# First products of the local attention in the linear attention's tail, and GpSimd's query low parts two heads ahead

## The reference, cut to what matters

```python
h = rmsnorm(x, norm_mix_g)
proj = h @ w_in            # linear attention q, k, v, r; local attention sq, sk, sv; two gates
o_a = rmsnorm(gla_chunked(gq, gk, gv, log_a)) * silu(gr)          # 4 heads of 128/256
q = partial_rope(rmsnorm(sq), cos, sin)                            # 16 heads of 64
k = partial_rope(rmsnorm(sk), cos, sin)                            # 4 key/value heads of 64
o_b = swa_sink_attention(q, k, sv, sinks)                          # window of 128
x = x + (sigmoid(gate_a) * (o_a @ w_a) + sigmoid(gate_b) * (o_b @ w_b)) @ w_out
# expert layer, 8 heads: the 16 best of 128 + 128 keys, then the 16 best of their 256 sums
qp = rmsnorm(x) @ w_pq
s_top, i_top = top_k(qp . sub_keys, 16)
best, pos = top_k(s_top[0][:, None] + s_top[1][None, :], 16)
x = x + sum_over_chosen(softmax(best) * gelu(x . u[idx]) * v[idx])
```

## Time and profile before

| | |
|---|---|
| median of three runs | 3020.08 us (3020.02 to 3022.21) |
| the profiled execution | 3024.87 us, its span 3023.1 us |
| mean granted clock of TensorE | 0.974 |
| TensorE busy | 2831.7 us (94%) |
| VectorE busy | 1832.2 us (61%) |
| ScalarE busy | 1207.7 us (40%) |
| GpSimd busy | 664.7 us (22%) |

### The profile page before, as it was taken

One profiled execution on the slowest core, in us unless ns is written; L12 is line 12 of the kernel. 1 busy time (PEld: TensorE's weight loads), 2 busy tenths in 40 slices (PEclk: granted clock), 3 DMA queues, 4 the chain that ended last, 5 costly groups with the idle time before them and its releaser, 6 DMA issues. The chain is left out here.

```text
span 3023.1 us, 39247 instructions
## 1 busy us (share of the span) xinstructions
PE 2831.7 (94%) x14634; PEld 2440.4 (81%) x14634; DVE 1832.2 (61%) x3340; ACT 1207.7 (40%) x2121; POOL 664.7 (22%) x400
## 2 busy tenths in 40 slices
PE   7989989989989999898999999899969988999998
PEld 6889558788989989897888888788757767888877
DVE  4434643369988888676788887644924554344432
ACT  3433642333337767332333333467424442222221
POOL 0013210023332333364232332043022310000000
PEclk9999999999999999999999999999979999999999
DMA  3202112344347988899999999467365531322232
GB/s 126 84 21 80 51 58 88 139 137 141 127 129 258 314 303 311 322 400 367 353 360 354 362 359 353 177 200 217 125 192 157 142 138 48 114 96 96 97 105 70
DMA packets 251468, 572.34 MB, mean 189 GB/s; under 512 B 43616, under 2 KB 152032, under 8 KB 222272
## 3 DMA queue, kind: packets, MB, share of 16 engines
q1 hardware_dynamic: 212160, 426.56, 42.1%
q0 software_dynamic: 36864, 134.23, 11.4%
q10 hardware_dynamic: 2304, 9.70, 0.9%
HBM read 486.38 MB, written 84.02 MB: 189 GB/s over the span
## 5 line engine op out<-in xcount | busy, mean ns | idle before, releaser
L44 PE MATMUL pe_ps<-hh,pe_uh 128*128 128x384 f32 x1024 | 349.8, 342 | 16.1 <-issue 13.6
L46 PE MATMUL pe_ps<-hh,pe_ul 128*128 128x384 f32 x1024 | 344.1, 336 | 0.0
L45 PE MATMUL pe_ps<-hl,pe_uh 128*128 128x384 f32 x1024 | 344.0, 336 | 0.0
L44 PE MATMUL pe_ps<-pe_vh,pe_whi 128*128 128x512 f32 x768 | 300.1, 391 | 6.5 <-DVE pe_vl L1721 6.5
L45 PE MATMUL pe_ps<-pe_vl,pe_whi 128*128 128x512 f32 x768 | 299.8, 390 | 0.0
L46 PE MATMUL pe_ps<-pe_vh,pe_wlo 128*128 128x512 f32 x768 | 299.7, 390 | 0.0
L1546 POOL DMA_INDIRECT pe_gu<-in_u_rows,pe_urow x128 | 198.8, 1553 | 304.6 <-DVE pe_gu L1682 287.5
L1554 POOL DMA_INDIRECT pe_gv<-in_v_w,pe_vrow x128 | 158.6, 1239 | 332.7 <-DVE pe_acc L1691 320.8
L44 PEld LDWEIGHTS pe_ps<-hh,pe_uh 128*128 128x128 f32 x1024 | 193.8, 189 | 18.2 <-issue 17.8
L1682 DVE SCALAR_TENSOR_TENSOR pe_gu<-pe_gu,pe_xs 128x1024 f32<-128x1024 f32 x128 | 155.0, 1218 | 86.1 <-DMA pe_gu<-in_u_rows,pe_urow 85.7
L45 PEld LDWEIGHTS pe_ps<-hl,pe_uh 128*128 128x128 f32 x1024 | 193.9, 189 | 0.3
(11 more groups left out here) (595 smaller groups left out, 6986.5 us busy)
## 6 DMA issues: line engine op xcount, KB each, us to landing
xu<-in_u_w SPq DMA_DIRECT2D x64, 1024.0 KB, 6.3
pe_v_raw<-in_v_w SPq DMA_DIRECT2D x64, 1024.0 KB, 8.5
hidden_scratch<-pe_hs SPq DMA_DIRECT2D x64, 384.0 KB, 8.5
gate_scratch<-pe_stage SPq DMA_DIRECT2D x24, 1024.0 KB, 11.2
pe_hw<-hidden_scratch SPq DMA_DIRECT2D x64, 384.0 KB, 4.6
pe_gate<-gate_scratch SPq DMA_DIRECT2D x64, 384.0 KB, 5.3
gf_raw<-in_gdn_w SPq DMA_DIRECT2D x16, 1024.0 KB, 6.8
gb_pk<-pk_scratch SPq DMA_DIRECT2D x64, 256.0 KB, 2.8
```

The source lines that it names most:

```text
L44: pe.matmul(out, lh, rh, start=start, stop=False)
L45: pe.matmul(out, lh, rl, start=False, stop=False)
L46: return pe.matmul(out, ll, rh, start=False, stop=stop)
```

## The change

- `gla`: it gets the banks (`ps`) of the local attention instead of its own. Behind the last head's products TensorE waits for the next phase's high weights (`nxt.w_hi`) and makes the products with them (`swa_high`: 16 a token tile) of three tiles, then the transposes, then the fourth tile's. SyncE also loads the raw weights of the local attention's head 1 into the one raw buffer, when head 0's are split on both engines.
- `swa_heads`: project(0) makes only the products with the low weights; project(1) makes its 64 products with the high weights before it waits for the low ones, then 32 with these. Head 2's raw weights have a buffer of their own (`sh_raw2`, in memory that the attention's output takes later) and a semaphore of their own, and are issued first in the phase, ahead of the small tables. Head 3's are loaded when head 1's are split.
- `peer`, GpSimd: the low part of head 1 first; then for head h the candidate sums, the low part of head h+2, the one-hot product.
- `peer`, VectorE: the low part of expert block 2h+3 goes behind the pick and ahead of the candidates' search (before, it stood behind the search in heads 0 to 6, and ahead of the pick in head 7). In head 7 block 19's, which stood behind the pick of head 7, goes ahead of the comparison.

```diff
@@ gla
             @block.sync
                 sp.wait_ge(w_lo, 2 * GLA_H)
                 sp.dma_start(nxt.raw[:], nxt.src).then_inc(nxt.raw_in, 16)
+                sp.wait_ge(nxt.w_hi, 1)
+                sp.wait_ge(nxt.w_lo, 1)
+                sp.dma_start(nxt.raw[:], nxt_src).then_inc(nxt.raw_in, 16)
...
                 steps(pe, GLA_H, step)
-                turn(GLA_H * NT)
+                pe.wait_ge(nxt.w_hi, 1)
+                for n in range(NT):
+                    swa_high(pe, ps, hh, hl, nxt.wh, n)
+                    if n == 2:
+                        turn(GLA_H * NT)
+def swa_high(pe, ps, hh, hl, wh, n):
+    rows = slice(n * P, (n + 1) * P)
+    for k in range(KD):
+        pe.matmul(ps[:, n, 0:SWA_COLS], hh[:, k, rows], wh[:, k, :], start=k == 0, stop=False)
+        pe.matmul(ps[:, n, 0:SWA_COLS], hl[:, k, rows], wh[:, k, :], start=False, stop=False)
@@ swa_heads
-        raw = first.raw
+        raw = [first.raw, first.raw, nc.alloc_sbuf_tensor_at("sh_raw2", [P, KD, SWA_COLS], F32, offset=spare), first.raw]
...
-                sp.dma_start(raw[:], w_dram[1]).then_inc(raw_in, 16)
+                sp.dma_start(raw[2][:], w_dram[2]).then_inc(other_in, 16)
...
-                for h in range(2, SWA_KV):
-                    sp.wait_ge(w_hi, h)
-                    sp.wait_ge(w_lo, h)
-                    sp.dma_start(raw[:], w_dram[h]).then_inc(raw_in, 16)
+                sp.wait_ge(w_hi, 2)
+                sp.wait_ge(w_lo, 2)
+                sp.dma_start(raw[3][:], w_dram[3]).then_inc(raw_in, 16)
...
                 def project(h):
                     pe.wait_ge(w_hi, h + 1)
+                    if h == 1:
+                        for n in range(NT):
+                            pe.wait_ge(pj_ok, n + 1)
+                            swa_high(pe, ps, hh, hl, wh[1], n)
                     pe.wait_ge(w_lo, h + 1)
...
+                            else:
+                                last = pe.matmul(ps[:, n, 0:SWA_COLS], hh[:, k, rows], wl[h][:, k, :], start=False, stop=k == KD - 1)
@@ peer, gpsimd
+                low_q(1)
                 for h in range(PEER_H):
-                    if h + 1 < PEER_H:
-                        pool.wait_ge(w_hi, h + 2)
-                        pool.tensor_tensor(wl[:], raw[:], wh[:].bitcast(F32), ALU.subtract).then_inc(w_lo, 1)
                     pool.wait_ge(m2, h + 1)
                     pool.tensor_tensor(cand[:], ...)
+                    if h + 2 < PEER_H:
+                        low_q(h + 2)
                     pool.wait_ge(eq_ok, h + 1)
@@ peer, vector
                     last.then_inc(x2, 1)
-                    if h == PEER_H - 1:
-                        low_u(2 * h + 3, 2 * h + 3)
                     if h:
                         pick(h - 1)
+                    low_u(2 * h + 3, 2 * h + 3)
...
                     last.then_inc(cx, 1)
-                    if h < PEER_H - 1:
-                        low_u(2 * h + 3, 2 * h + 3)
+                    if h == PEER_H - 1:
+                        low_u(2 * h + 5, 2 * h + 5)
...
                 pick(PEER_H - 1)
-                low_u(2 * PEER_H + 3, 2 * PEER_H + 3)
```

More of the change, by code:

```diff
@@ L223, in _, with gla @@
                     last.then_inc(turned, 1)
-def gla(nc, hh, hl, oa, ident, drams, first, nxt):
+def gla(nc, ps, hh, hl, oa, ident, drams, first, nxt, nxt_src):
     w_dram, glr_dram, gk2_dram, bgk_dram, gain_dram, tri_dram, reset_dram = drams
@@ L529, in _, with swa_heads @@
                 steps(pe, GLA_H, step)
-                turn(GLA_H * NT)
-def swa_heads(nc, ps, hh, hl, qT, kT, v, ident, drams, first, gates):
+                pe.wait_ge(nxt.w_hi, 1)
[8 more added lines that the diff above has]
+        pe.matmul(ps[:, n, 0:SWA_COLS], hl[:, k, rows], wh[:, k, :], start=False, stop=False)
+def swa_heads(nc, ps, hh, hl, qT, kT, v, ident, drams, first, gates, spare):
     w_dram, qg_dram, kg_dram, cos_dram, sin_dram = drams
@@ L550, in swa_heads @@
         ro = [ph.sb(f"ro{i}", [P, NT, NH, ROPE_HALF]) for i in range(4)]
+        other_in = ph.sem("other_in")
         names = ("small_in proj sq_ok pj_ok v_ok ss_ok ms_ok root_ok rs_ok normed gained r1 roped dup "
@@ L580, in split @@
                 def split(h):
-                    act.wait_ge(raw_in, 16 * (h + 1))
+                    if h == 2:
+                        act.wait_ge(other_in, 16)
+                    else:
+                        act.wait_ge(raw_in, 32 if h == 1 else 48)
                     if h >= 2:
                         act.wait_ge(proj, (h - 1) * NT)
-                    act.activation(wh[h % 2][:], raw[:], ACT.Copy).then_inc(w_hi, 1)
+                    act.activation(wh[h % 2][:], raw[h][:], ACT.Copy).then_inc(w_hi, 1)
                 def keep(h):
@@ L616, in _ @@
                     pool.wait_ge(w_hi, h + 1)
-                    pool.tensor_tensor(wl[h % 2][:], raw[:], wh[h % 2][:].bitcast(F32), ALU.subtract).then_inc(w_lo, 1)
+                    pool.tensor_tensor(wl[h % 2][:], raw[h][:], wh[h % 2][:].bitcast(F32), ALU.subtract).then_inc(w_lo, 1)
                 pool.wait_ge(gates.w_hi, 1)
@@ L653, in project @@
                     pe.wait_ge(w_hi, h + 1)
+                    if h == 1:
+                        for n in range(NT):
+                            pe.wait_ge(pj_ok, n + 1)
+                            swa_high(pe, ps, hh, hl, wh[1], n)
                     pe.wait_ge(w_lo, h + 1)
                     for n in range(NT):
-                        if h:
+                        if h >= 2:
                             pe.wait_ge(pj_ok, (h - 1) * NT + n + 1)
@@ L659, in project @@
                         for k in range(KD):
-                            last = mm3(pe, ps[:, n, 0:SWA_COLS], (hh[:, k, rows], hl[:, k, rows]),
-                                       (wh[h % 2][:, k, :], wl[h % 2][:, k, :]), k == 0, k == KD - 1)
+                            if h >= 2:
+                                last = mm3(pe, ps[:, n, 0:SWA_COLS], (hh[:, k, rows], hl[:, k, rows]),
+                                           (wh[h % 2][:, k, :], wl[h % 2][:, k, :]), k == 0, k == KD - 1)
+                            else:
+                                last = pe.matmul(ps[:, n, 0:SWA_COLS], hh[:, k, rows], wl[h][:, k, :], start=False, stop=k == KD - 1)
                         last.then_inc(proj, 1)
@@ L1525, in _, with low_q @@
             def _(pool):
+                def low_q(h):
+                    pool.wait_ge(w_hi, h + 1)
+                    pool.tensor_tensor(wl[:], raw[:], wh[:].bitcast(F32), ALU.subtract).then_inc(w_lo, 1)
+                low_q(1)
                 for h in range(PEER_H):
-                    if h + 1 < PEER_H:
-                        pool.wait_ge(w_hi, h + 2)
-                        pool.tensor_tensor(wl[:], raw[:], wh[:].bitcast(F32), ALU.subtract).then_inc(w_lo, 1)
                     pool.wait_ge(m2, h + 1)
@@ L3069, in program @@
             branches = nc.sbuf_base
+            pair = ExitStack()
             oa = (sb("oah", [P, KD, T], F32R, mix), sb("oal", [P, KD, T], F32R, mix))
-            gla(nc, hh, hl, oa, ident, [a[n] for n in ("gla_w", "glr_w", "gk2", "bgk", "gla_gain", "tri", "reset")], gla_first, sh_first)
+            ps = pair.enter_context(nc.psum_tensor("swa_ps", [P, 8, 512], F32))
+            gla(nc, ps, hh, hl, oa, ident, [a[n] for n in ("gla_w", "glr_w", "gk2", "bgk", "gla_gain", "tri", "reset")], gla_first, sh_first,
+                a["swa_w"][1])
+            spare = nc.sbuf_base
             ob = (sb("obh", [P, KD, T], F32R, mix), sb("obl", [P, KD, T], F32R, mix))
@@ L3076, in program @@
                 v = sb("v", [P, SWA_KV, NT, HD], F32, sw)
-                ps = sw.enter_context(nc.psum_tensor("swa_ps", [P, 8, 512], F32))
-                swa_heads(nc, ps, hh, hl, qT, kT, v, ident, [a[n] for n in ("swa_w", "qg", "kg", "cos", "sin")], sh_first, gate_first)
+                swa_heads(nc, ps, hh, hl, qT, kT, v, ident, [a[n] for n in ("swa_w", "qg", "kg", "cos", "sin")], sh_first, gate_first, spare)
                 swa_attend(nc, ps, hh, hl, qT, kT, v, ob, ga, ident, (a["mask"], a["sinks"], a["mrg_w"]), gate_first, mrg_first)
+            pair.close()
             mt = (sb("mth", [P, KD, T], F32R, mix), sb("mtl", [P, KD, T], F32R, mix))
```

1 line of the change is left out of this document (removed).

## The result

Over five runs of each on one chip the changed kernel has a median of 3001.99 us (3000.12 to 3007.74), the kernel before 3020.08 (3015.49 to 3022.40). The ratio of the runs is 0.9945, with a 95% interval of 0.9934 to 0.9956, which is 13.3 to 19.9 us less. On a second chip it was 3005.15 against 3021.70, 0.9939 [0.9927, 0.9952]. The forecast was 3002.3. The part on the sum comes back to this.

What follows compares the result with a forecast made beforehand. TensorE, busy for 94% of the span, was taken as the bound, so only its gaps and half-speed matmuls pay. Gains of 7.2 + 6.5 + 4.1 = 17.8 us off the median of 3020.08 gave 3002.3 us, range 2997 to 3010.

Steps and rivals of the forecast that it cites:

- The tail fill: Linear attention's tail: 64 of head 0's 96 products fill TensorE's 6.5 us gap; the next stage opens 2.2 us later.
- What is late next: Local attention: late small tables and GpSimd's low part hold head 0's vector chain; its transposes wait 3.4 us.
- Rival A: Local attention: small tables don't hold VectorE, so no 3.4 us wait; 2998.9 us in all, chance 0.12.
- Part 1: Linear attention's tail and local attention's heads: products made early gain 7.2 us, bounds 5.6 and 10.6.
- gain 7.2 us: Local attention: head 0's transposes start at about 255.1 instead of 262.26.
- lower bound of 5.6: Local attention: gain if the clock falls in the new 3.4 us gap, which costs 1.6 us.
- Part 2: Top-k stretch: query low parts two heads ahead remove five gaps before projections, 6.46 us; head period 29.62 us.
- Part 3: End of top-k: VectorE's moved expert low parts remove block 19's gap, leaving 2.6 us at block 20; gain 4.1 us.
- Rival C: Top-k: GpSimd's low part holds VectorE's 256-candidate searches, 22.8 us lost; 3025 us in all, chance 0.03.
- Rival B: Gate stage gives back 4.1 us, or VectorE's 0.7 us slack is missing; 3006.4 or 3009 us, chance 0.22.
- The sum: Whole kernel: gains of 7.2, 6.5 and 4.1 us make 17.8 us, giving a median of 3002.3 us.

Runs made afterwards that it cites:

- tables_first: Changed kernel with the local attention's small tables issued ahead of the third head's raw weights: 2997.85 us, 0.9921 of the kernel before.
- after_again: The changed kernel run again without an edit, on the first chip of the experiments: 3005.15 us, 0.9939 of the kernel before.
- tail_only: Kernel before with only the edits of the linear attention's tail and the local attention's heads: 3016.34 us, 0.9981 of the kernel before.
- block20: Changed kernel with VectorE's low part of expert block 20 moved ahead of the last pick: 3001.01 us, 0.9933 of the kernel before.
- lowq_only: Kernel before with only GpSimd's new order in the expert layer, VectorE's expert low parts in their old places: 3014.33 us, 0.9974 of the kernel before.
- peer_only: Kernel before with only the expert layer's edits (GpSimd's order and VectorE's expert low parts): 3010.18 us, 0.9962 of the kernel before.
- one_buffer: Changed kernel without the third head's own raw buffer, its weights loaded into the one buffer behind the small tables: 3001.72 us, 0.9932 of the kernel before.

## Why the prediction was right, point by point

**The tail fill, right.** The stage was to open 2.2 us later, and did 2.15; head 0's low products (5.82 us from 230.00) and head 1's 96 followed without a wait, and the transposes were ready to run at 252.46, forecast 251.7 and 0.5 of offset.

**What is late next, right in place and cause.** Forecast, with the offset: tables at 241.3, rotary product held from 246.6, transposes at 255.6 behind a gap of 3.4. Measured: 241.26, 246.61 and 255.11, gap 2.65. From the end of GpSimd's part to the transposes it was 1.9 us and not 2.4. Rival A is refuted by the same rows: the sine table's landing releases VectorE's first reduction, and the wait is there. tables_first shows what the tables' place costs.

**Part 1's size, wrong by its own bound.** The step that failed is "gain 7.2 us": the prediction named the lower bound of 5.6, for a clock that falls in the new gap, and did not take it. It fell. The first scores of the local attention start at 304.73 against 310.20, 6.0 us earlier without the offset, against 7.2, and 6.1 in each of the three other executions of the same code (after_again, tail_only, block20). In tables_first they start at 300.86, 3.9 earlier for a wait that is 2.3 shorter: the other 1.6 us is the clock's part, as the bound had it.

**What no step had: the clock at the next stages.** From 5.6 us at the merge the gain shrinks to 2.9 at the expert layer (6.1 and 3.4 without the offset), with the same instructions. TensorE's timeline at the merge, of before, of the changed kernel and of tables_first:

```profile
422.75 0.76 PE L44 MATMUL mrg_ps<-oah,mrg_first_wh 128*128 128x512 f32 x1 [3.04 <-PEq L80]
431.88 0.47 PE L44 MATMUL mrg_ps<-hh,mrg_wh 128*128 128x512 f32 x1 [0.63 <-DVE mrg_wl L949]
```
```profile
417.14 0.47 PE L44 MATMUL mrg_ps<-oah,mrg_first_wh 128*128 128x512 f32 x1 [3.04 <-PEq L80]
426.45 0.77 PE L44 MATMUL mrg_ps<-hh,mrg_wh 128*128 128x512 f32 x1 [3.59 <-DVE mrg_wl L973]
```
```profile
413.39 0.77 PE L44 MATMUL mrg_ps<-oah,mrg_first_wh 128*128 128x512 f32 x1 [3.05 <-PEq L80]
422.60 0.47 PE L44 MATMUL mrg_ps<-hh,mrg_wh 128*128 128x512 f32 x1 [0.68 <-DVE mrg_wl L973]
```

The same 3.04 or 3.05 us between the stages end in a clock of 0.50 in the first and the third (a matmul of 0.76 or 0.77 us), and of 1.00 in the second (0.47). Full speed brings nothing there: the second product's weights come 9.1 to 9.3 us after the opening in each, by a transfer, a copy and a subtraction. The fast first product waits 3.59 us for them, and now the clock falls behind that wait, on work that nothing hides. The output projection opens 3.97 us earlier than before instead of 5.61; it opened at full clock before (0.47) and at half in the changed kernel (0.77), and its normalized result is 2.94 earlier. In tables_first the lead is 9.4 us at the merge and 9.2 at the expert layer: nothing lost. From the merge to the expert layer it is 198.7 to 199.0 us in all four executions of the changed kernel's code, and 196.2 to 196.4 in before, lowq_only, peer_only and tables_first, so this loss repeats. But the edit's text does not fix the clock: block20 ran the changed kernel's code and kept full speed through the local attention, so that it was 6.3 us ahead of before at the expert layer and not 3.4 (without offsets). That the half-speed stretches lie elsewhere is seen; what decides after gaps of equal length which way the clock goes, these runs leave open.

**Part 2, right, 1.0 us too small.** The five gaps went. The head period was to be 29.62 and is 29.38; lowq_only brought 7.5 us against 6.46. The mis-sized term is the sum of the gaps: the ends of matmuls are modelled in the profile, and a gap was worth 30.82 - 29.38 = 1.44 us of period and not 1.20. The starts in the trace of before showed it:

```profile
740.07 0.33 PE L45 MATMUL pe_ps<-hl,pe_uh 128*128 128x384 f32 x1
740.24 0.34 PE L46 MATMUL pe_ps<-hh,pe_ul 128*128 128x384 f32 x1
741.81 0.47 PE L44 MATMUL pe_ps<-hh,pe_first_wh 128*128 128x512 f32 x1 [1.23 <-issue]
```

Two products follow each other 0.17 us apart, and over this gap 1.57: 1.40 lost, where the brackets say 1.23. The moved low part cost VectorE's shift 0.99 instead of 0.19 us, 0.8 against at most 1.3 allowed, and the slack came out at 0.84 against 0.7. One reading was off and changed nothing: ScalarE's split ends at 755.90, which is 16.7 us before the projection at 772.63, and not "some 22".

**Part 3, right.** Forecast 4.1 with a new gap of 2.6 at block 20; lowq_only and peer_only are 4.4 apart in the top-k column, and the gap is 2.61. Here the clock stayed at 1.00.

**Rival C, wrong.** The search steps over 256 candidates lie within GpSimd's low part (749.83 to 754.46) and take 0.42 us (751.89), as they do ahead of it. The two-input product and the shift beside GpSimd are held, the searches not. The Trainium skill ("SBUF — State Buffer", section "Who interferes with whom") read on operands alone would have held these too; the measurement decides against that reading.

**Rival B, not seen.** From the index transposes to the v products it is 471.5 and 470.8 us, against 472.3. That stage spreads by more than B's 4.1 us, and in peer_only it took 474.7, so the profiles alone don't refute B; but peer_only's 11.9 us at top-k are there in its medians (11.5). In the window of the earlier trace rows TensorE is busy for 24.21 of 25 us instead of 22.74 (and for 24.06 in 1035.4 to 1060.4, where the changed kernel is at the same work):

```profile
1050.00:1075.00 25.00, 24.21 (x162) 1.00 0.83 284
```

**The sum.** At the index transposes the changed kernel is 14.6 us ahead (15.1 without the offset), not 17.8: 2.9 from the tail and 11.7 from top-k. The other 8.4 us between the two profiled executions (0.8 in the gate stage, 7.6 in the rest) lie where no code changed and where ten profiles spread as widely. The median's 18.1, with an interval of 13.3 to 19.9, holds both 14.6 and 17.8. That the forecast came within 0.3 us of the median is luck: one term is 4.3 too large (3.8 without the offset), two together are 1.1 too small, and the rest is within what the comparison can't tell.

## What to carry to other kernels

- Filling a tail with the next stage's work pays as far as what the next stage then needs first: follow the second engine's chain, down to its smallest table, and issue small transfers that gate a chain ahead of large ones that have slack.
- A low-priority product on one in-order engine (here the split of later weights) belongs where its own wait is over, not behind a product that waits for another engine.
- Count a stall by a difference of starts over a whole period, and judge an edit of a few us by milestones in the trace: the total carries several us that unchanged stages add or take. A milestone needs a second execution of the same code beside it as well: here one differed by 2.9 us.

## What the runs showed of the hardware

- After gaps of 3.04 or 3.05 us at the same place the granted clock was 0.50 in the kernel before and in tables_first, and 1.00 in the changed kernel; after one of 2.65 us it fell, after one of 2.61 us at block 20 it did not. Going from one to the other moved up to 1.6 us per place.
- Two executions of the same code differed in it: in 402 to 408 the granted clock was 0.72 in the changed kernel and 1.00 in block20.
- A 16 KB table took 8.0 us from issue to landing behind 1.5 MB on the same queue, 6.4 us ahead of it (tables_first), and 5.5 us with no such transfer before or behind it (one_buffer): the large transfer explains 2.5 of the 8.0 us.
- Beside GpSimd's subtraction VectorE's two-input products of 128x160 lasted 6.8 us instead of 0.33 and a one-input shift 0.99 instead of 0.19, while its search over 256 columns kept its 0.42 us.
- In a stage that opens on a DMA of weights, a faster clock before the weights are in was worth nothing, and behind the wait that it opened (3.59 us at the merge instead of 0.63) the clock was at 0.50.
